# Two blocks on one core: mLSTM values centred per token and head where they leave the accumulators

## The reference, cut to what matters

```
def layernorm32(x, eps):
    xc = x32 - jnp.mean(x32, axis=-1, keepdims=True)
    return xc * lax.rsqrt(jnp.mean(xc * xc, axis=-1, keepdims=True) + eps)
...
    num = (w_inter * einsum(c_state, qc) + einsum('bhts,bhse->bhte', scores, vc))
    h = num / jnp.maximum(jnp.abs(den), jnp.exp(-m_t))[..., None]
...
    h = layernorm32(h, LN_EPS)            # per token and head, over its 256 elements
    return sigmoid(o_pre) * h * head_g
```

## Time and profile before

| | |
|---|---|
| runs | 1891.7, 1892.67, 1892.9 us (median 1892.67) |
| span of the profiled execution | 1892.0 us (the profile gives no other time of it) |
| PE busy | 1878.6 us, 99% of the span |
| DVE, ACT, POOL busy | 1021.4, 794.1, 230.8 us |
| granted TensorE clock, mean | 0.998 |

### The profile page before, as it was taken

One profiled execution on the slowest core, in us unless ns is written; L12 is line 12 of the kernel. 1 busy time (PEld: TensorE's weight loads), 2 busy tenths in 40 slices (PEclk: granted clock), 3 DMA queues, 4 the chain that ended last, 5 costly groups with the idle time before them and its releaser, 6 DMA issues.

```text
span 1892.0 us, 21295 instructions
## 1 busy us (share of the span) xinstructions
PE 1878.6 (99%) x8689; PEld 1556.2 (82%) x8689; DVE 1021.4 (54%) x1291; ACT 794.1 (42%) x1064; POOL 230.8 (12%) x267
## 2 busy tenths in 40 slices
PE   9999999999999999999999999999999999999998
PEld 7888888888888887888888888888888888888886
DVE  5434434348354666664434444566574877775335
ACT  5423222236444566433223322566674434443224
POOL 2000001201300111140000022110113200000111
PEclk9999999999999999999999999999999999999999
DMA  4432322342241322423332223343323232233231
GB/s 162 163 104 89 100 101 89 101 160 95 83 136 64 101 80 87 146 90 100 100 101 89 100 90 101 114 119 96 105 104 118 102 105 95 90 107 103 91 122 56
DMA packets 55122, 196.85 MB, mean 104 GB/s; under 512 B 7192, under 2 KB 7448, under 8 KB 53872
## 3 DMA queue, kind: packets, MB, share of 16 engines
q1 hardware_dynamic: 49184, 170.42, 27.3%
q0 software_dynamic: 5120, 24.02, 3.7%
q10 hardware_dynamic: 720, 1.05, 0.2%
HBM read 181.28 MB, written 13.13 MB: 103 GB/s over the span
## 4 chain that ended last, share of the span: by engine, by line
PE 96%; ACT 2%; DVE 1%; issue 0%; DMA 0%; POOL 0%; SPq 0%; ACTq 0%; DVEq 0%
PE psum L1859 95%; ACT at L875 1%; ACT tml L875 0%; DMA x<-in_xT 0%; DVE tml L1222 0%; DVE x L1662 0%; ACT x L875 0%; PE psum L2261 0%; DVE at L1595 0%; ACT wh L875 0%; ACT pp L875 0%; DVE wl L1228 0%; DVE az L1225 0%; DVE tm L1470 0%; ACT az L875 0%
## 5 line engine op out<-in xcount | busy, mean ns | idle before, releaser
L1859 PE MATMUL psum<-xh,wh 128*128 128x512 f32 x1760 | 694.6, 395 | 1.1 <-DVE wl L1228 0.8
L1859 PE MATMUL psum<-xh,wl 128*128 128x512 f32 x1760 | 685.3, 389 | 0.0
L1859 PE MATMUL psum<-xl,wh 128*128 128x512 f32 x1760 | 685.3, 389 | 0.0
L1228 DVE TENSOR_TENSOR wl<-wraw,wh 128x1024 fp32r<-128x1024 f32 (+1 forms) x314 | 399.2, 1278 | 387.4 <-ACT wh L875 386.3
L875 ACT ACTIVATE wh<-wraw 128x1024 fp32r<-128x1024 f32 (+1 forms) x314 | 325.7, 1047 | 362.8 <-PE psum L1859 361.5
L1859 PEld LDWEIGHTS psum<-xh,wh 128*128 128x128 f32 x1760 | 330.6, 188 | 76.6 <-issue 7.9
L1859 PEld LDWEIGHTS psum<-xl,wh 128*128 128x128 f32 x1760 | 330.7, 188 | 69.9 <-issue 3.4
L1859 PEld LDWEIGHTS psum<-xh,wl 128*128 128x128 f32 x1760 | 330.5, 188 | 69.6
L1712 POOL TENSOR_TENSOR ssq<-x 128x512 f32<-128x512 f32 x5 | 5.2, 1037 | 713.8 <-DVE x L1307 454.2
L1859 PE MATMUL psum<-wh,xh 128*128 128x512 f32 (+1 forms) x256 | 88.2, 345 | 0.1
L1859 PE MATMUL psum<-wh,xl 128*128 128x512 f32 (+1 forms) x256 | 86.0, 336 | 0.0
(11 more groups left out here) (336 smaller groups left out, 2204.5 us busy)
## 6 DMA issues: line engine op xcount, KB each, us to landing
wraw<-in_w_ffn SPq DMA_DIRECT2D x86, 512.0 KB, 3.2
wraw<-in_w_down SPq DMA_DIRECT2D x44, 512.0 KB, 3.2
wraw<-in_w_up SPq DMA_DIRECT2D x44, 512.0 KB, 3.5
wraw<-in_w_qg SPq DMA_DIRECT2D x28, 512.0 KB, 3.4
wraw<-in_w_att SPq DMA_DIRECT2D x24, 512.0 KB, 3.2
wraw<-in_w_dn SPq DMA_DIRECT2D x22, 512.0 KB, 3.3
wraw<-in_w_zu SPq DMA_DIRECT2D x16, 512.0 KB, 3.3
wraw<-in_w_zv SPq DMA_DIRECT2D x8, 512.0 KB, 3.6
```

Source lines behind the costliest of these rows:

```text
L1228: return e.tensor_tensor(dst, src, hi.bitcast(F32), ALU.subtract)
L1859: return e.matmul(dst, lhsT, rhs, start=start, stop=stop, skip_group_check=skip)
```

## The change

- `vev`: ACT copies each token group's two 256-wide halves (one per head) from PSUM to fp32 scratch (`tm(6 + i)`), scaled by `rc`, and its accumulator gives each half's sum.
- A new step `vc`: DVE turns the two sums into minus the means (a 128x2 operation); ACT writes `vh` = scratch + (minus mean) in two halves; DVE writes `vl` = (scratch + minus mean) - `vh` in two halves. For c = 0 the four `vc` steps stand right behind `vev`, ahead of units 98 and on. For c = 1 they stand at (103, 3) (`C0 C1`) and (104, 0) (`C2 C3`).
- T.0, T.1 and T.2 are gone. T.4 also lets ACT copy the added squares to an fp32r high part `rr[:, 1]` and DVE make the low part `thl`; T.5 is two fp32r matmuls with `onesr` in place of one fp32 matmul with `ones`. Some T steps stand elsewhere in `MIX_AT`.
- Waits on the values' banks go to the copies' signals; H.7 of heads 0 and 2 waits for the low parts.

```diff
-    (103, 1): "H0.7", (103, 2): "T0.0 H1.m", (103, 3): "T0.1", (104, 0): "T0.2", (105, 3): "T0.3 T0.4",
+    (103, 1): "H0.7", (103, 2): "H1.m", (103, 3): "C0 C1", (104, 0): "C2 C3", (105, 3): "T0.3 T0.4",
-    (110, 2): "H1.7", (110, 3): "G0 G1 T1.0", (111, 0): "T1.1",
-    (111, 1): "T1.2 T1.3", (111, 2): "T1.4 H2.m", (111, 3): "T1.5", (112, 0): "T1.6",
+    (110, 2): "H1.7", (110, 3): "G0 G1", (111, 0): "T1.3",
+    (111, 1): "T1.4", (111, 2): "H2.m", (111, 3): "T1.5", (112, 0): "T1.6",
-    (116, 3): "H2.6", (117, 3): "G3 H2.7", (118, 0): "T2.0", (118, 3): "T2.1", (119, 0): "T2.2", (119, 1): "T2.3",
-    (119, 2): "T2.4 H3.m", (119, 3): "T2.5", (120, 0): "T2.6", (122, 0): "H3.0 T2.7",
+    (116, 3): "H2.6", (117, 3): "G3 H2.7", (118, 3): "T2.3", (119, 0): "T2.4",
+    (119, 2): "H3.m", (119, 3): "T2.5", (120, 0): "T2.6", (122, 0): "H3.0 T2.7",
-    (126, 0): "T3.0", (126, 3): "T3.1", (127, 0): "T3.2", (127, 1): "T3.3", (127, 2): "T3.4", (127, 3): "T3.5",
-    (128, 0): "T3.6", (129, 0): "T3.7", (129, 3): "G6 G7",
+    (126, 3): "T3.3", (127, 0): "T3.4", (127, 2): "T3.5",
+    (127, 3): "T3.6", (128, 3): "T3.7", (129, 3): "G6 G7",
...
         for i in range(4):
             step("vev", c, i)
+        for i in range(0 if c else 4):
+            step("vc", c, i)
@@ ACT, vev @@
-                act(vh[:, i, 512 * c:512 * c + 512], bank(TG_BANKS["v", c][i]), ACT.Copy,
-                    scale=rc[:, i:i + 1]).then_inc(v_a.sem, 1)
+                b, m = bank(TG_BANKS["v", c][i]), vmean(c, i)
+                act(tm(6 + i)[:, 0:256], b[:, 0:256], ACT.Copy, scale=rc[:, i:i + 1], accum_out=m[:, 0:1])
+                act(tm(6 + i)[:, 256:512], b[:, 256:512], ACT.Copy, scale=rc[:, i:i + 1],
+                    accum_out=m[:, 1:2]).then_inc(v_a.sem, 1)
+            elif kind == "vc":
+                e.wait_ge(*v_d.at(c, i, "m"))
+                act(vh[:, i, 512 * c:512 * c + 256], tm(6 + i)[:, 0:256], ACT.Identity, bias=m[:, 0:1])
+                act(vh[:, i, 512 * c + 256:512 * c + 512], tm(6 + i)[:, 256:512], ACT.Identity,
+                    bias=m[:, 1:2]).then_inc(v_a.sem, 1)
@@ ACT, T.4, behind the second square @@
+                    e.wait_ge(*t_d.at(h, "sq"))
+                    act(rr[:, 1, :], tm(4), ACT.Copy).then_inc(t_a.sem, 1)
@@ DVE, vev, then vc @@
-                e.wait_ge(*v_a.at(c, i))
-                stt(vl[:, i, r], bank(TG_BANKS["v", c][i]), rc[:, i:i + 1], vh[:, i, r].bitcast(F32), ALU.mult,
+                e.wait_ge(*v_a.at(c, i, "t"))
+                e.tensor_scalar(m, m, -1.0 / 256, None, ALU.mult).then_inc(v_d.sem, 1)
+                e.wait_ge(*v_a.at(c, i, "h"))
+                stt(vl[:, i, r0], tm(6 + i)[:, 0:256], m[:, 0:1], vh[:, i, r0].bitcast(F32), ALU.add, ALU.subtract)
+                stt(vl[:, i, r1], tm(6 + i)[:, 256:512], m[:, 1:2], vh[:, i, r1].bitcast(F32), ALU.add,
                     ALU.subtract).then_inc(v_d.sem, 1)
@@ DVE, T.0 and T.2, then T.4 behind the sum of the squares @@
-                    e.tensor_tensor(t4, h0, h1, ALU.add).then_inc(t_d.sem, 1)
-                    stt(h0, bD, -1.0 / 256, h0, ALU.mult, ALU.add).then_inc(t_d.sem, 1)
-                    stt(h1, bD, -1.0 / 256, h1, ALU.mult, ALU.add).then_inc(t_d.sem, 1)
+                    e.wait_ge(*t_a.at(h, "h"))
+                    low(thl[:, :], t4, rr[:, 1, :]).then_inc(t_d.sem, 1)
@@ PE, T.1 and T.5 @@
-                if s == 1:
-                    mm(bank(7), ones[:, :], tm(4)).then_inc(t_p.sem, 1)
-                elif s == 5:
-                    mm(bank(7), ones[:, :], tm(4)).then_inc(t_p.sem, 1)
+                if s == 5:
+                    e.wait_ge(*t_a.at(h, "h"))
+                    mm(bank(7), onesr[:, :], rr[:, 1, :], True, False)
+                    e.wait_ge(*t_d.at(h, "l"))
+                    mm(bank(7), onesr[:, :], thl[:, :], False, True).then_inc(t_p.sem, 1)
```

More of the change, by code:

```diff
@@ L109, in short_steps @@
             yield ("gated", j)
+        elif c == "C":
+            yield ("vc", 1, int(n))
         elif c == "M":
@@ L477, in _build @@
     tm2 = sb("tm2", [128, 6, 512], F32, ml)
+    thl = sb("thl", [128, 512], F32R, ml)
     ml.close()
@@ L546, in wide, with vmean @@
         return c.unsqueeze(2).to_broadcast([128, 4, 128])
+    def vmean(c, i):
+        return ccol[:, 16 + 4 * i + 2 * c:18 + 4 * i + 2 * c]
     wis = vl[:, 3, :].rearrange("p (k m) -> p k m", m=128)
@@ L708, in _build @@
                                        7: [(h, "h1"), (h, "dd")]}.get(s, []))
[L709 to L712, removed]
+    t_p = sig("s_t_p", T=lambda h, s: {5: [(h, "cs")]}.get(s, []))
+    t_a = sig("s_t_a", T=lambda h, s: {3: [(h, "sq0")], 4: [(h, "sq1"), (h, "h")], 6: [(h, "ln"), (h, "R")]}.get(s, []))
+    t_d = sig("s_t_d", T=lambda h, s: {4: [(h, "sq"), (h, "l")], 6: [(h, "u")], 7: [(h, "n0"), (h, "n1")]}.get(s, []))
     og_d = sig("s_og_d", ogev=lambda j: [(j, "o"), (j, "g"), (j, "og")])
@@ L1035, in _ @@
                 e.wait_ge(*unit_done(97 + 4 * c))
-                act(vh[:, i, 512 * c:512 * c + 512], bank(TG_BANKS["v", c][i]), ACT.Copy,
-                    scale=rc[:, i:i + 1]).then_inc(v_a.sem, 1)
+                if c == 0:
+                    e.wait_ge(*sv_g.at(7))
+                else:
+                    e.wait_ge(*v_d.at(0, i, "l"))
+                b, m = bank(TG_BANKS["v", c][i]), vmean(c, i)
[3 more added lines that the diff above has]
+            elif kind == "vc":
+                c, i = a
+                m = vmean(c, i)
+                e.wait_ge(*v_d.at(c, i, "m"))
+                act(vh[:, i, 512 * c:512 * c + 256], tm(6 + i)[:, 0:256], ACT.Identity, bias=m[:, 0:1])
+                act(vh[:, i, 512 * c + 256:512 * c + 512], tm(6 + i)[:, 256:512], ACT.Identity,
+                    bias=m[:, 1:2]).then_inc(v_a.sem, 1)
             elif kind == "H":
@@ L1437, in _ @@
             elif kind == "vev":
+                pass
+            elif kind == "vc":
                 c, i = a
-                e.wait_ge(*v_a.at(c, i))
-                r = slice(512 * c, 512 * c + 512)
-                stt(vl[:, i, r], bank(TG_BANKS["v", c][i]), rc[:, i:i + 1], vh[:, i, r].bitcast(F32), ALU.mult,
+                m = vmean(c, i)
+                e.wait_ge(*v_a.at(c, i, "t"))
+                e.tensor_scalar(m, m, -1.0 / 256, None, ALU.mult).then_inc(v_d.sem, 1)
+                e.wait_ge(*v_a.at(c, i, "h"))
+                r0, r1 = slice(512 * c, 512 * c + 256), slice(512 * c + 256, 512 * c + 512)
+                stt(vl[:, i, r0], tm(6 + i)[:, 0:256], m[:, 0:1], vh[:, i, r0].bitcast(F32), ALU.add, ALU.subtract)
+                stt(vl[:, i, r1], tm(6 + i)[:, 256:512], m[:, 1:2], vh[:, i, r1].bitcast(F32), ALU.add,
                     ALU.subtract).then_inc(v_d.sem, 1)
@@ L1464, in _ @@
                 h0, h1, t4, bD = hn[:, 2 * h, :], hn[:, 2 * h + 1, :], tm(4), bank(7)
[L1465 to L1469, removed]
-                    e.tensor_tensor(t4, h0, h1, ALU.add).then_inc(t_d.sem, 1)
-                elif s == 2:
-                    e.wait_ge(*t_p.at(h, "sum"))
-                    stt(h0, bD, -1.0 / 256, h0, ALU.mult, ALU.add).then_inc(t_d.sem, 1)
-                    stt(h1, bD, -1.0 / 256, h1, ALU.mult, ALU.add).then_inc(t_d.sem, 1)
-                elif s == 4:
+                if s == 4:
                     e.wait_ge(*t_a.at(h, "sq1"))
                     e.tensor_tensor(t4, t4, tm(5), ALU.add).then_inc(t_d.sem, 1)
+                    e.wait_ge(*t_a.at(h, "h"))
+                    low(thl[:, :], t4, rr[:, 1, :]).then_inc(t_d.sem, 1)
                 elif s == 6:
@@ L1786, in _ @@
                     e.wait_ge(*mg_g.at(j - 1))
+                else:
+                    e.wait_ge(*v_d.at(1, 3, "l"))
                 e.dma_start(tm(9 if j < 7 else 0), mgd[:, j, :]).then_inc(s_mgb[j], 16)
@@ L1910, in _ @@
                         if p == 0:
-                            e.wait_ge(*v_d.at(0, 2))
+                            e.wait_ge(*v_a.at(0, 2, "t"))
                         elif p == 1:
-                            e.wait_ge(*v_d.at(0, 3))
-                            e.wait_ge(*v_d.at(1, 0))
+                            e.wait_ge(*v_a.at(1, 0, "t"))
                         else:
@@ L2051, in _ @@
                     else:
-                        e.wait_ge(*v_d.at(0, 0))
+                        e.wait_ge(*v_a.at(0, 0, "t"))
                         e.wait_ge(*sel_d.at("lo"))
@@ L2083, in _ @@
                     for j in range(4):
-                        if h == 0:
-                            e.wait_ge(*v_d.at(1, j))
+                        if h % 2 == 0:
+                            e.wait_ge(*v_d.at(h // 2, j, "l"))
                         r = slice(OFF[j], OFF[j] + 512 - 128 * j)
```

12 lines of the change are left out of this document (5 added, 7 removed).

## The result

The changed kernel takes 1900.2 us (median of 5 runs, 1898.5 to 1900.7); before it is 1892.67 (1891.7 to 1893.1). The ratio is 1.0037 with a 95% interval of 1.0026 to 1.0047: slower by 7.5 us. The predicted time was 1898.9, its range 1895.3 to 1901.3. The rival in which the clock falls had 1900.6.

The account below looks back on a forecast made before the run. PE, with 96% of the chain, was taken to bound the kernel. The terms 1.35 + 7.25 - 2.4 gave +6.2 us, so 1898.9 against the median of 1892.67, range 1895.3 to 1901.3.

Parts of the forecast that it names:

- The rival in which the clock falls: Units 106 and 107: first two waits' falls swallowed, one behind the third paid, at most 1.7 us; +7.9, 1900.6; chance 0.20.
- the likeliest case: Whole kernel, terms as worked without a clock fall: +6.2 us, 1898.9, own range 1897.3 to 1900.8; chance 0.60.
- PE's work: Norm's sums: fp32 matmuls removed or replaced by fp32r pairs, and T1.1's wait gone; at most 5.6 us saved.
- c = 0: Unit 100: copies and four `vc` steps of 1.9 us make `wl` late, so PE waits; +1.35 us (0.9 to 2.2).
- The rival in which steps take 1.5 or less: All eight `vc` steps: small operations issue closer, waits shrink by 3.2; +3.0 us, 1895.7; chance 0.12.
- c = 1's copies: Ahead of H0.3: eight copies delay ACT by 1.3 us, covered by about 1; nothing, or 0.5 if copies cost 0.49.
- C0 to C3: Units 106 and 107: three PE waits of 2.6, 2.9 and 2.7 us in one chain; +7.25 us, T0.1 included.
- Heads 1 to 3: Behind unit 107: T1.1 and T2.1 save, T1.5 and T2.5 save nothing, head 3 saves 0.2; -2.4 us (-1.9 to -3.6).
- With no wait and T1.5, T2.5 and T3's part lost: Rival, `vc` steps fit unit 106's cover: -5.6 us, or -3.9 with these losses, about 1888; chance 0.08.

Follow-up runs that it names:

- e4: Changed kernel's norm alone, values as in the kernel before, so the mean is subtracted nowhere: 1890.17 us, ratio 0.9988; profiled stretch -2.6 us against before.
- e8: e7 with T3.5 moved from (127, 2) to (127, 3): 1886.33 us, ratio 0.9965 to the kernel before.
- e7: e6 with T1.6 and T2.6 placed later, behind the next head's k evict: 1887.14 us, ratio 0.9968 to the kernel before.
- e1: Changed kernel with only the four `vc` steps of c = 0 moved behind the split of unit 100: 1898.28 us, ratio 1.0029 to the kernel before.
- e3: Changed kernel with DVE making all four means of a c before the first low part: 1895.17 us, ratio 1.0015 to the kernel before.
- e2: Changed kernel with C0 to C3 spread to (102, 2), (103, 0) and (103, 2): 1891.46 us, ratio 0.9995 to the kernel before.
- e5: Changed kernel plus 26 unread matmuls on constants in its three long PE waits (9, 9, 8): 1899.53 us, ratio 1.0034 to the kernel before.
- e10: Kernel before with the values' part alone (values centred, norm left as it was): 1902.21 us, ratio 1.0047 to the kernel before.
- e6: Changed kernel with the edits of e1 and e3, c = 1's steps and head 0's norm placed early: 1889.14 us, ratio 0.998 to the kernel before.

## Why the prediction was right, and where it was off

The direction, the places and the order of the waits were right; the time is 1.3 above the forecast, inside its range. On the stretch it is +7.94 against the +6.2 of the likeliest case, and 1.6 of these 1.7 are one term, the clock. The 1.3 on the medians is not the same count: the profiled execution has this fall and took 1899.12, only 0.2 above the forecast, because of its shorter start and end.

**PE's work.** Right in kind: the chain at T0.5 shows two matmuls 0.23 apart (638.59, 638.82, 639.06), as forecast. Its whole worth, 5.6, can't be had in this order of steps (e4: 2.6); with the waits moved away e8 has 6.5, more than 5.6, since e7 most likely also took away waits that before had at heads 2 and 3.

**c = 0.** Forecast +1.35, measured 1.32; taken away in e1. The timelines of ACT and DVE show the loop that the prediction described, here ahead of unit 100, and then what stood behind it in units 105 to 107:

```profile
566.05 0.91 ACT L882 ACTIVATE vh<-tm,ccol 128x256 fp32r<-128x256 f32 x2 [1.03 <-DVE ccol L1465]
567.00 0.88 DVE L1247 SCALAR_TENSOR_TENSOR vl<-tm,ccol,vh 128x256 fp32r<-128x256 f32 x2 [0.98 <-ACT vh L882]
567.79 0.16 DVE L1465 TENSOR_SCALAR ccol<-ccol 128x2 f32<-128x2 f32 x1
567.99 0.91 ACT L882 ACTIVATE vh<-tm,ccol 128x256 fp32r<-128x256 f32 x2 [1.03 <-DVE ccol L1465]
...
617.49 1.23 DVE L1250 TENSOR_TENSOR wl<-wraw,wh 128x1024 fp32r<-128x1024 f32 x1
...
623.79 1.28 DVE L1244 TENSOR_TENSOR tmpm<-psum,R 128x512 f32<-128x512 f32 x2
...
633.04 0.63 ACT L882 ACTIVATE rr<-tm 128x512 fp32r<-128x512 f32 x1 [0.76 <-DVE tm L1495]
...
634.64 1.28 ACT L878 ACT_TABLE_LOAD   x1
635.93 1.78 ACT L882 ACTIVATE att<-psum,ccol 128x512 f32<-128x512 f32 x4
```

One step takes 567.99 - 566.05 = 1.94 (1.9 was taken). ACT idles 1.03 of it and DVE 0.98: each waits for the other. The rival in which steps take 1.5 or less falls; with e3's order of operations they do.
The Trainium skill ("TensorE: Matmul & The Clock Gate", Architectural detail: the array is 16x 32x32) says that ACT and DVE work strictly first in, first out; the trace agrees, as the split of unit 106 at 617.49 stands behind two `vc` steps that it has nothing to do with.

**c = 1's copies.** Eight copies, which for c = 0 start every 0.45, were to be covered, and H0.3 has no wait (588.82, 24 matmuls in 3.97): as forecast.

**C0 to C3.** Forecast +7.25 up to behind T0.5; from the table it is 9.14 - 1.32 - 0.42 = 7.4. `wl` of unit 106 ends at 617.49 + 1.23 = 618.72 (forecast 618.3; with the 1.35 by which unit 100 is late, less the 1.04 by which this execution is earlier, 618.6). The k evict starts 7.96 later than before on this count (623.79 - 560.47 against 616.87 - 561.51), forecast 1.35 + 6.45 = 7.8. The exponentials end at 635.93 + 1.78 = 637.71. All three waits are one chain, as e2 shows: 8.6 us go when its steps are moved, the clock's 1.6 among them.

**Heads 1 to 3.** T1.1's wait is gone and T2.1 saves its matmul; H2.3 and H3.3 stand 0.45 longer, forecast 0.42, and take back T1.5 and T2.5. For head 3 nothing is left (H3.3 at +7.96, the end at +7.94) where 0.2 was forecast: DVE's last splits come at 801.32 instead of 794.44, and PE stands 0.67 ahead of unit 132. This small term was set too high by 0.2.

**The clock.** This is the term that the forecast had wrong: the likeliest case left the fall out, and the rival that has it got 0.20. All its parts were in the text, the three waits, the fall of the earlier trace rows behind a wait of 1 us, the swallowing of the first two and 1.7 for the third, where e5 puts 1.6. The rival's sum, +7.9, is what the stretch measured, +7.94; that it fits so closely is luck, as other terms were off by 0.1 to 0.2 both ways. Looking back, the four kernels of this study that have such a row of waits (changed, e1, e3, e10) all show a fall at the last of them; from one fall in the trace of before this couldn't be told. Nor could it be told at which wait it would come: e1 has none behind 2.65 and 2.71. Of the falls forecast as possible, the one at the first wait came and was indeed swallowed (H1.3's wait 1.25 instead of 2.9); behind the second none came.
The Trainium skill ("TensorE: Matmul & The Clock Gate", HAM oscillation) warns that a TensorE left idle between its matmuls falls to half its clock, and the trace agrees in kind: 1.00 to 0.50, that is 2.4 to 1.2 GHz, at waits of 2.65 and 2.41 us. By that section of the Trainium skill alone, though, waits this short would not have been expected to bring a fall. The measurement decides.

**Slips in the sums of the rivals.** None changes the forecast. With smaller steps the wait at unit 100 can shrink by its 1.35 only, not by 4 x 0.4 = 1.6, so that rival had +3.25 and not +3.0. With no wait and T1.5, T2.5 and T3's part lost, the terms of the text give 0.87 + 0.42 + 2.4 = 3.7 and not 3.9; e6, which has no wait up to H2.3, measured 3.7. And the range's upper end, 1901.3, takes in the clock's rival at its likeliest, 1900.6, but not with its bounds: the likeliest case's own upper bound plus 1.7 is 1902.5.

What stays open: where the other runs of the changed kernel have their falls, and whether each has one at the third wait. The profiled one, with a mean clock of 0.997, has. One fall of 3.4 us lowers the mean by 3.4 x 0.5 / 1897 = 0.0009, so the three runs with a mean of 0.994 (1900.2 to 1900.65 us) have, by this estimate, some three more; they leave no trace to read them in. So the 1.6 stands for the profiled execution, and the clock's share of the 7.5 us between the medians may be another.

## What to carry to other kernels

A step in which two in-order engines take turns costs the sum of both and the hops, 1.94 us here for 0.91 and 0.88 of work, and what it delays is not its own result but the next thing in each queue that the bottleneck wants: place such steps by the distance between each queue's next due result and its need, or batch one engine's half of them (e3). Nearly the same instructions (the fastest order needs four table loads fewer) were worth +7.5 us in one order and -6.5 us in another. And when a forecast has the TensorE stand for as long as here, a fall of its clock belongs in the sum unless some later wait swallows it: five of the seven waits of 2.4 us and more in these traces had one.

## What the runs showed of the hardware

- The granted clock fell to 0.50 at PE waits of 2.65 us (0.2 before its end) and 2.41 (1.4 behind its end) in the changed kernel, and during waits of 2.41 (e1, e3) and 3.69 (e10). It did not at waits of 2.65 and 2.71 in e1, nor at any of 1.75 or less between 560 and 814. A fall lasted 3.4 us in the changed kernel and e1, and 6.8 in e3 and e10.
- With 26 matmuls on constants within the waits (e5) the trace has no fall, and the stretch was 1.6 us shorter. This is one execution.
- An accumulating copy of 256 columns from PSUM on ACT, with its read of the accumulator, comes every 0.45 us (560.47, 560.93, 561.38).
- The place of one step, T.6, decided over two function table loads of 1.28 us each in a head's part, and over the wait of PE behind them (e6 to e7: 1.9 us for two heads).
